# Moving the split weight tiles by 192 or 64 bytes against the streams of TensorE

## The reference, cut to what matters

```python
# first block, twice (two layers)
gq, gk, gv, gr, glr, fq, fk, fv, ff = split(rms_norm(h) @ w_in[i])
h = h + concat([o_gla, o_fox]) @ w_out[i]           # linear attention, forgetting attention
h = h + (silu(g) * u) @ w_down[i]                   # u, g: causal conv of rms_norm(h) @ w_up[i]
# second block, once
q, k, v, qi, ki, wi, cu, cb, cc, ga, gb = split(rmsnorm(h) @ w_in_2[0])
y_attn = dsa_attention(q, k, v, qi, ki, wi) @ w_attn_out_2[0]     # top-132 keys of each query
y_conv = (cb * short_conv(cc * cu)) @ w_conv_out_2[0]
h = h + (sigmoid(ga) * y_attn + sigmoid(gb) * y_conv) @ w_out_2[0]
h = h + (silu(f @ w_gate_2[0]) * (f @ w_up_2[0])) @ w_down_2[0]   # f: rmsnorm(h)
out = rmsnorm(h)[:, 16:]
```

## Time and profile before

| what | value |
|---|---|
| median of three executions | 2210.01 us |
| the profiled execution's own time | 2211.83 us |
| its span, first to last instruction | 2210.1 us |
| granted TensorE clock, mean | 0.999 of full speed |
| PE busy | 2184.6 us, 99% of the span, 15711 matmuls |
| weight loads (PEld) busy | 2003.0 us, 91% |
| DVE busy | 1424.6 us, 64% |
| ACT busy | 1069.0 us, 48% |
| POOL busy | 149.3 us, 7% |

### The profile page before, as it was taken

The page is one execution under the profiler, slowest core; times in us unless marked ns, Lnnn a source line. Parts: engine busy times, 40 slices in busy tenths (PEclk is TensorE's granted clock), DMA queues, the critical chain, the costliest instruction groups (busy, mean ns, idle before and its releaser), DMA issues.

```text
span 2210.1 us, 39479 instructions
## 1 busy us (share of the span) xinstructions
PE 2184.6 (99%) x15711; PEld 2003.0 (91%) x15711; DVE 1424.6 (64%) x2661; ACT 1069.0 (48%) x2027; POOL 149.3 (7%) x245
## 2 busy tenths in 40 slices
PE   9999999999999999999999999999999999999998
PEld 7799999999997899998899889978899888998997
DVE  5356689559744466898398566869444465863664
ACT  5356556347533465555276534223244444652652
POOL 4111011100000011100000010110000000000001
PEclk9999999999999999999999999999999999999999
DMA  6656778775335546664455262777512222543651
GB/s 200 191 148 162 186 187 235 214 228 177 130 95 156 162 114 160 188 185 147 125 174 160 81 191 96 202 202 206 155 68 67 67 95 87 157 159 118 182 174 51
DMA packets 104738, 336.15 MB, mean 152 GB/s; under 512 B 14967, under 2 KB 19037, under 8 KB 102253
## 3 DMA queue, kind: packets, MB, share of 16 engines
q1 hardware_dynamic: 90460, 227.30, 31.3%
q0 software_dynamic: 13376, 105.03, 20.4%
q10 hardware_dynamic: 720, 1.31, 0.2%
HBM read 331.46 MB, written 102.79 MB: 196 GB/s over the span
## 4 chain that ended last, share of the span: by engine, by line
PE 91%; DVE 4%; ACT 2%; issue 1%; POOL 1%; POOLq 0%; ACTq 0%; DVEq 0%
PE G L1486 54%; PE G L1523 17%; PE G L1602 7%; PE X L1523 3%; PE X L1823 1%; DVE wL L2500 1%; PE X L1910 1%; PE X L1775 1%; PE X L1799 1%; ACT wH L1963 1%; PE X L1894 1%; PE X L1879 1%; PE X L1562 1%; PE X L1866 0%; PE X L1729 0%
## 5 line engine op out<-in xcount | busy, mean ns | idle before, releaser
L1963 ACT ACTIVATE wH<-raw 128x512 fp32r<-128x512 f32 (+3 forms) x741 | 491.8, 685 | 434.0 <-PE G L1486 353.7
L2500 DVE TENSOR_TENSOR wL<-raw,wH 128x512 fp32r<-128x512 f32 (+3 forms) x741 | 556.5, 764 | 217.7 <-ACT wH L1963 214.3
L1486 PE MATMUL G<-aH,wH 128*128 128x264 f32 (+3 forms) x1744 | 445.0, 318 | 3.1 <-DVE aL L2513 2.4
L1486 PE MATMUL G<-aH,wL 128*128 128x264 f32 (+3 forms) x1744 | 426.8, 307 | 0.0
L1486 PE MATMUL G<-aL,wH 128*128 128x264 f32 (+3 forms) x1744 | 426.6, 307 | 0.0
L1486 PEld LDWEIGHTS G<-aH,wH 128*128 128x128 f32 (+1 forms) x1744 | 283.3, 188 | 23.1 <-issue 2.8
L1486 PEld LDWEIGHTS G<-aH,wL 128*128 128x128 f32 (+1 forms) x1744 | 281.5, 187 | 16.2
L1486 PEld LDWEIGHTS G<-aL,wH 128*128 128x128 f32 (+1 forms) x1744 | 281.7, 188 | 13.1 <-issue 0.2
L1523 PE MATMUL G<-seven,wH 128*128 128x256 f32 (+2 forms) x1152 | 212.0, 283 | 2.9 <-DVE wL L2500 1.6
L2661 DVE TENSOR_TENSOR hT<-G,hT 128x528 f32<-128x528 f32 (+1 forms) x83 | 58.0, 699 | 199.3 <-PE G L1486 199.1
L1523 PEld LDWEIGHTS G<-seven,wH 128*128 128x128 f32 x1152 | 177.1, 188 | 5.4 <-issue 3.3
(11 more groups left out here) (412 smaller groups left out, 3968.9 us busy)
## 6 DMA issues: line engine op xcount, KB each, us to landing
raw<-weights SPq DMA_DIRECT2D x179, 512.0 KB, 4.0
weight_sums<-weights POOLq DMA_DIRECT2D x72, 704.0 KB, 6.5
raw<-weight_sums SPq DMA_DIRECT2D x192, 256.0 KB, 2.9
raw<-weights SPq DMA_DIRECT2D x145, 256.0 KB, 2.9
raw<-weights SPq DMA_DIRECT2D x48, 704.0 KB, 4.1
weight_sums<-weight_sums POOLq DMA_DIRECT2D x24, 704.0 KB, 4.8
weight_sums<-weights POOLq DMA_DIRECT2D x24, 512.0 KB, 5.2
weight_sums<-weights POOLq DMA_DIRECT2D x24, 448.0 KB, 5.3
```

What stands on the lines that cost most here:

```text
L1486: done = e.matmul(m.pair(i)[0:M, bank, 0:n], a[:, k, 0:M], b[:, kx, lo - t0:lo - t0 + n], start=(k == 0 and c == 0), stop=(k == nk - 1 and ...
L1963: e.activation(m.high(i)[:, c], m.raw(i)[:, c], ACT.Copy).then_inc(s.w_hi, 1)
L2500: e.tensor_tensor(m.low(i)[:, c], m.raw(i)[:, c], m.high(i)[:, c].bitcast(F32), ALU.subtract).then_inc(s.w_lo, 1)
```

## The change

A new function `behind` gives each split tile an offset of 0, 16 or 48 columns, which is 0, 64 or 192 bytes. `places()` adds it to the tile's column in `wH` and `wL`. Tiles whose streams are `REAL` get 48, the token-major tiles of 256 columns (gk) get 48, the token-major tiles of 512 columns (gv, fv, vv) get 16, and all others get 0: the `FULL` and `TAPS` tiles, the seven tiles, and the one tile right behind a run of seven tiles. `wH` and `wL` grow by 64 columns each. `places()` also books `SIZE[i]` columns for a tile where it booked a whole slot of 1408 before.

```diff
+BEHIND = 64
...
+def behind(i):
+
+    role = ROLE[i]
+    if role[0] == "seven" or i and ROLE[i - 1][0] == "seven":
+        return 0
+    if role[0] in TOKEN_MAJOR:
+        return 48 if role[0] == "gk" else 16
+    return 48 if parts_of(role) is REAL else 0
...
-    last, k = [-1] * (NW * WMAX), 0
+    last, k = [-1] * (NW * WMAX + BEHIND), 0
...
-            at, k, n = 512 * k, (k + 1) % 5, n + n % 2
+            at, k, n = 512 * k + behind(i), (k + 1) % 5, n + n % 2
         else:
-            at, n = WMAX * (n % NW), n + 1
+            at, n = WMAX * (n % NW) + behind(i), n + 1
         place[i] = at
-        size = 512 if role[0] == "seven" else WMAX
+        size = SIZE[i]
...
-        self.wH = sb("wH", [128, NW * WMAX], F32R)
-        self.wL = sb("wL", [128, NW * WMAX], F32R)
+        self.wH = sb("wH", [128, NW * WMAX + BEHIND], F32R)
+        self.wL = sb("wL", [128, NW * WMAX + BEHIND], F32R)
```

## The result

The changed kernel takes 2214.96 us (median of 10 runs, 2213.87 to 2216.28) against 2209.69 us before (median of 10, 2209.46 to 2212.13). The ratio is 1.0023, 95% interval 1.0013 to 1.0033: slower by 5.3 us. The forecast was 2199 us, with a range from 2186 to 2214 us.

The account below looks back on a forecast made before the run. PE was taken to bound the kernel, busy 99% of the span. Gains of 8.6 us at line 1486, 2.0 us in token-major 512-column tiles and 0.7 us in gk made 11.3 us, giving 2199 us, range 2186 to 2214 us.

Parts of the forecast that it names:

- the price of an offset at 512 columns: 512-column steps moved to 192 bytes: 3.4 ns less than at 0, forecast between 2 and 5 ns, chance 0.45.
- the 256-column rows: Profile rows 5 to 7: 120.0 ns a step at offset 0, 117.8 and 113.1 ns at 64 bytes.
- one excess of 13.3 ns a matmul at offset 0: 256-column steps over 106.7 ns at offset 0; claimed one amount per matmul, not per column, as at 512 columns.
- 8.6 us of gain at line 1486: 2523 matmuls of 512 columns moved to 192 bytes, 3.4 ns less each.
- 2.0 us in the token-major tiles: 576 token-major matmuls of 512 columns moved to 192 bytes, 3.4 ns less each.
- 0.7 us in gk: 192 token-major matmuls of 256 columns moved to 64 bytes, 3.4 ns less each.
- the last tile's 0: 66 matmuls of 256 columns moved to 192 bytes; 0.2 us either way, counted as 0.
- rival "slower": Every 512-column step lengthens by 3 ns as weight load may meet stream at 192 bytes: 9.3 us, 2219 us; chance 0.18.
- rows 10 and 11: 400-column scores of line 1894: 1030 ns at head 2, 1039 ns at head 3 with offsets 192, 64, 192; 3 ns longer each.
- the control tiles: Tiles right behind a run of seven, keeping offset 0: 33 matmuls each, claimed to still step by 226.7 ns.
- addresses can't matter: What the skill's rule of two independent PE read ports would mean: a sum of 0; rows 5 to 7 disagree.
- supply: Work feeding PE, DVE's evacuations next late; with PE 1.5% quicker DVE would be at 79%, so nearly all gain arrives.

Follow-up runs that it names:

- narrow-streams kernel: Changed kernel with the 68 one-stream 512-column tiles cut to 256, 320, 384 or 448 columns at 0, 64 or 192 bytes, others at 0; no time given.
- room without offsets: Changed kernel with every offset set back to 0, keeping the extra columns and the booking by `SIZE`; 2209.64 us, ratio to before 1.0000.
- 4-byte map: Changed kernel with 68 512-column tiles 4 to 28 bytes either side of 0, and second-block 256-column seven tiles at all sixteen offsets; 2219.04 us.

## Why the prediction was wrong

The step of the prediction that failed is the price of an offset at 512 columns. "I take the 256-column rows, since their excess at offset 0 is that of the 512-column rows and these scores come singly behind other work": minus 3.4 ns a step was carried from 256 to 512 columns. It is plus 2.3 ns there (226.7 to 229.0 in tiles that run unbroken), about plus 1 ns in the token-major tiles, and nothing in dq and ga. The ground given for it, one excess of 13.3 ns a matmul at offset 0, does not hold from width to width: the narrow-streams kernel has 13.2 ns at 320, 14.3 at 384 and 17.0 at 448 columns at that same offset. And even where the excess is the same, at 256, 320 and 512 columns, 64 bytes gain, do nothing and lose.

The terms: 8.6 us of gain at line 1486 came as 4.6 us of loss, 2.0 us in the token-major tiles as 0.6 us of loss, 0.7 us in gk as 0.4 to 0.5 us of gain, the last tile's 0 as 0.1 us of gain.

The rival "slower", which had been given 0.18, was right in its sign and in its place, the 512-column steps, though not in every one of them. Its price was 3 ns a step and 9.3 us in all, from rows 10 and 11; 2.3 ns in unbroken tiles and 5.1 us in all were measured. Those rows were the only ones with 0 and 192 both in them, and were set aside for being few. That they came near is in part luck: they have 400 columns, and in the narrow-streams kernel 192 bytes is better than 0 on either side of that, by 0.8 ns at 384 and by 3.5 ns at 448 columns. The mechanism that the rival named, a load that meets the stream, was not shown. Without a row at that width and at that offset, nothing gave the price a sign; even chances for both would have said so.

What held: PE bounds the kernel and waits for nothing new; the order and the waits are untouched; the shift of everything behind wH costs nothing (room without offsets: ratio 1.0000); gk gains; the control tiles step as before (227.9 ns before and 227.8 after, slow starts included). Whether supply would have hidden a gain was not tested, since there was none at 512 columns.

Two rules of the Trainium skill were weighed. Its page "SBUF — State Buffer", section "Who interferes with whom", makes PE's two read ports independent; the prediction took from it that addresses can't matter. That does not agree with 226.9 ns at 0 and 233.4 ns at 64 bytes in tiles of one kind; the measurement decides, and whether the ports make the difference was not shown. The Trainium skill's page "TensorE: Matmul & The Clock Gate", section "Back-to-back issue gap", gives columns over 2.4 plus 2.5 ns for the gap of a matmul by itself, without the share of a weight load, which is 215.8 ns here. No tile at any of the 28 offsets tried at 512 columns comes near it; the lowest tile has 226.7.

## What to carry to other kernels

An offset between the weights and the stream was worth about 3% of a matmul's step here, but it has to be measured at the width that it is meant for: 64 bytes gained 3 ns at 256 columns and lost twice as much at 512. A map costs one run, with the tiles of one shape at different offsets side by side in the same program, and is read from the steps in the trace, not from the time. It is read tile by tile: where the tiles of one offset differ by 6 ns, their mean says little. Where all of a shape already steps alike to a nanosecond and the trace holds no other offset of that shape, the price of moving it has no known sign.

## What the runs showed of the hardware

The loads are not what gets longer. From 1500 to 1575 us a weight load beside a 512-column stream takes 187.8 ns before, 187.8 at 192 bytes and 187.0 at 64 bytes, while the modelled duration of the matmul goes from 389.0 to 391.4 and 394.0 ns. At 192 bytes the three products no longer agree; before each has 389 and at 64 bytes each has 394. One row of before, the three at 192 bytes, one at 64 bytes:

```profile
L1486 PE MATMUL G<-aH,wH 128*128 128x512 f32 x55 | 21.4, 389 | 0.0
...
L1498 PE MATMUL G<-aH,wH 128*128 128x512 f32 x56 | 22.1, 394 | 0.0
L1498 PE MATMUL G<-aH,wL 128*128 128x512 f32 x56 | 22.0, 392 | 0.0
L1498 PE MATMUL G<-aL,wH 128*128 128x512 f32 x56 | 21.7, 388 | 0.0
...
L1498 PE MATMUL G<-aH,wH 128*128 128x512 f32 x53 | 20.9, 394 | 0.0
```

Matmuls of one shape at one offset can have two levels, and a kernel can fall into either. At 512 columns that showed at 16 bytes (226.7 and 233.5 ns) and 4 bytes short of the stream (226.7 and up to 234.1); at 256 columns it is plainest. The seven tiles of the second block keep 64 bytes in every kernel but that of the 4-byte map. Where the kernel before ran them at 113.1 ns, the changed one runs the same tiles at (40.00 + 0.28) / 342 = 117.8 ns (line 1535 alone, busy time and counts of PE and PEld, clock, DMA):

```profile
2093.00:2133.00 40.00, 40.00 (x342) 40.00 (x341) 1.00 0.60 178
```

and the kernel with 512 columns at 64 bytes is back at 113.1 ns there:

```profile
2103.00:2143.00 40.00, 40.00 (x356) 40.00 (x355) 1.00 0.60 177
```

In all eleven traces in which these tiles keep 64 bytes, the level changes only in the first few matmuls after PE has stopped for a wait or has run another shape, and then stays until the next such place. The 1512 steps together sum to 0.5 us less than before in the changed kernel, 1.7 us less in the room-only one and 3.7 us less in the one at 64 bytes, with no change to them. That this also spreads the times of one kernel over 2 to 4 us is a guess, and was not shown.

What stays open: why 0 is the one offset at which every unbroken tile of 512 columns keeps the short step, why other widths have other best offsets, and how load, stream and step make the rhythm.
